# Conditioning vectors from VectorE sums over transposed weights, in a two-layer mLSTM / Mamba-2 / MoE step

## What is computed

```python
mod = silu(c) @ ada_w[l] + ada_b[l]      # (6 * 1024), for c and for c_ctx; l = 0, 1
x <- LayerNorm(ALPHA * x + gate * sublayer(x * (1 + scale) + shift))
```

## Time and profile before

| | us |
|---|---|
| median of 3 runs | 1399.95 |
| lowest, highest | 1393.66, 1410.97 |
| the profiled execution | 1397.49 |
| its span (first to last instruction) | 1395.7 |

### The profile page before, as it was taken

One profiled execution on the slowest core, in us unless ns is written; L12 is line 12 of the kernel. 1 busy time (PEld: TensorE's weight loads), 2 busy tenths in 40 slices (PEclk: granted clock), 3 DMA queues, 4 the chain that ended last, 5 costly groups with the idle time before them and its releaser, 6 DMA issues.

```text
span 1395.7 us, 15980 instructions
## 1 busy us (share of the span) xinstructions
PE 1263.1 (90%) x5974; PEld 687.4 (49%) x5974; DVE 526.4 (38%) x1263; ACT 352.2 (25%) x763; POOL 159.2 (11%) x222
## 2 busy tenths in 40 slices
PE   6999998999999999897779999999999999899573
PEld 3555555554566444643224555555666544644221
DVE  0344336432222122721013446557887222541014
ACT  1322332221310011211014132233555310311011
POOL 5000210000000000004003101003233000002201
PEclk9999997999999999899898999999999999899797
DMA  9566203337354552599949473234444266399934
GB/s 375 211 227 234 83 0 133 109 121 248 112 212 152 179 181 75 225 418 421 402 170 360 152 303 113 77 98 139 149 134 138 76 274 253 126 400 421 420 154 152
DMA packets 75416, 287.10 MB, mean 206 GB/s; under 512 B 7644, under 2 KB 18140, under 8 KB 61388
## 3 DMA queue, kind: packets, MB, share of 16 engines
q1 hardware_dynamic: 53472, 233.07, 44.5%
q10 hardware_dynamic: 17468, 37.67, 7.6%
q0 software_dynamic: 4400, 15.35, 2.8%
HBM read 258.16 MB, written 27.90 MB: 205 GB/s over the span
## 4 chain that ended last, share of the span: by engine, by line
PE 73%; DMA 9%; DVE 9%; issue 5%; ACT 3%; SPq 1%; ACTq 0%; POOL 0%; DVEq 0%; POOLq 0%
PE bank L586 21%; PE bank L608 12%; PE bank L747 7%; DMA arena<-in_moe_gu 4%; PE bank L959 4%; PE bank L767 3%; PE bank L559 3%; DMA ring<-in_ada_w 3%; PE bank L1155 3%; DVE arena L2478 2%; PE bank L995 2%; PE bank L890 1%; PE bank L987 1%; PE bank L850 1%; PE bank L546 1%
## 5 line engine op out<-in xcount | busy, mean ns | idle before, releaser
L586 PE MATMUL bank<-hT,ring 128*128 128x384 f32 x896 | 300.9, 494 | 3.8 <-ACT hT L1514 1.7
L586 PEld LDWEIGHTS bank<-hT,ring 128*128 128x128 f32 x896 | 169.9, 193 | 122.5 <-issue 13.6
L608 PE MATMUL bank<-ring,arena 128*128 128x512 f32 (+1 forms) x512 | 173.4, 605 | 2.1 <-DVE arena L2086 2.1
L747 PE MATMUL bank<-arena,hT 128*64 128x512 f32 x416 | 105.8, 628 | 35.8 <-DMA arena<-in_moe_gu 24.3
L608 PEld LDWEIGHTS bank<-ring,arena 128*128 128x128 f32 (+1 forms) x512 | 72.6, 194 | 92.9 <-issue 86.8
L1920 DVE SCALAR_TENSOR_TENSOR arena<-arena,par 128x388 f32<-128x388 f32 x160 | 99.8, 624 | 5.6
L1155 PE MATMUL bank<-hT,ring 128*128 128x384 f32 x256 | 97.2, 505 | 0.2 <-ACT arena L1528 0.2
L747 PEld LDWEIGHTS bank<-arena,hT 128*64 128x64 f32 x416 | 37.1, 144 | 92.9 <-issue 87.3
L559 PE MATMUL bank<-ring,csil 128*32 128x256 f32 x768 | 64.3, 450 | 20.0 <-DMA ring<-in_ada_w 12.4
L1461 POOL TENSOR_TENSOR arena<-arena 128x192 f32<-128x192 f32 x64 | 43.0, 702 | 240.0 <-PE bank L1188 156.6
L959 PE MATMUL bank<-ring,arena 128*128 128x512 f32 x128 | 58.9, 620 | 0.9 <-ACT arena L1591 0.9
(11 more groups left out here) (412 smaller groups left out, 1625.3 us busy)
## 6 DMA issues: line engine op xcount, KB each, us to landing
arena<-in_moe_gu SPq DMA_DIRECT2D x56, 1024.0 KB, 14.6
ring<-in_ada_w SPq DMA_DIRECT2D x96, 512.0 KB, 5.7
arena<-in_moe_dn SPq DMA_DIRECT2D x28, 1024.0 KB, 11.9
ring<-in_b_w_in SPq DMA_DIRECT2D x40, 512.0 KB, 4.2
ring<-in_a_w_in SPq DMA_DIRECT2D x32, 512.0 KB, 3.6
ring<-in_moe_gu SPq DMA_DIRECT2D x12, 1024.0 KB, 14.1
arena<-acs_rows ACTq DMA_DIRECT2D x32, 384.0 KB, 3.6
yg<-arena ACTq DMA_DIRECT2D x18, 512.0 KB, 8.4
```

The lines of the kernel that those rows point to most:

```text
L586: last = mm(keys[j][1][:, 0:T], w[:, k, P * j:P * j + P], hT[:, 4 * half + k, :], start=half == 0 and k == 0, stop=half == 1 and k == 3, s ...
L608: last = mm(keys[t][1][p:p + tokens.shape[1], :], tokens, w[:, j, :], start=k == 0, stop=k == KE - 1, skip_group_check=True)
L747: last = mm(ps[CAP * u:CAP * u + CAP, :], m_hg[:, q % 2, P * k + CAP * u:P * k + CAP * u + CAP], v3(w[u][1], 4)[:, j, :], start=k == 0, st ...
```

## The change

40 of the 48 units leave TensorE. Units 0 to 7 (columns 0 to 15 of layer 0) stay. The other 80 column blocks of 128 come as slabs of kind "column", from a copy of the weights laid out so that partition p holds the 1024 weights of column 128*j + p. VectorE multiplies a slab with silu(c), kept in all partitions, and sums it with one `scalar_tensor_tensor` with accumulator per vector: two instructions of 128x1024 per slab, each waited for. No PSUM, no copy of rows, no turn. `biased` adds bias and 1 afterwards.

silu(c) and silu(c_ctx) in all partitions (128 x 2048, 1 MB) are loaded three times (`c_rows_at`) by a broadcast load, once to a free region of the arena and twice to hT, and ScalarE applies Silu in place (`c_silu`). For the second and third the load stands on SyncE's queue until the last z projection has read hT.

The 80 columns are summed in three places: 20 in the xu stage, two after each of ten convolutions; 28 in the down stage, in one go after `diagonals(0)`; 32 in the out stage, as 8, 6 and 18, with `diagonals(2)` between and the mean-square wait ahead of the last 18. Their slabs stand between those of TensorE in the same ring, and their slots come free by a semaphore of VectorE. `gate_rows(0)` moves from after the eighth down slab to after the third, `gate_rows(2)` to after the sixth out slab (banks 5 and 7).

```diff
+        c_free = region(3 * D, KE * T + KE * W_PAD)[0]
+        hT_free = hT.rearrange("p k t -> p (k t)")
+        c_places = [(v3(a[:, 0:2 * D], 2), a[:, 2 * D:3 * D]) for a in (c_free, hT_free, hT_free)]
...
+        for tile in range(KD):
+            add("ada", ada_w, tile)
+        for i in range(2 * KD):
+            add("xu", a_in, i // 2, (i % 2,))
+            if i == 1:
+                c_rows_at.append(len(slabs))
+            if i in (1, 2, 4, 5, 7, 8, 10, 11, 13, 14):
+                add_columns(2)
...
         for s in range(8):
             for kp in range(2):
+                if s == 1 and kp == 0:
+                    c_rows_at.append(len(slabs))
                 slabs.append(("down", a_dn[s // 4, 2 * (s % 4) + kp]))
+                if s < 6:
+                    add_columns(4 if (s, kp) in ((1, 0), (2, 1)) else 2)
             prefetch(0, 4 + s)
...
+        rest_at = len(slabs) + RING
...
+        c_rows_at.append(len(slabs))
         for s in range(16):
             slabs.append(("out", b_dn[s // 8, s % 8]))
+            if s < 12:
+                add_columns(4 if s in (1, 3, 5, 7) else 2)
             if s >= 6:
                 prefetch(1, s - 6)
...
+        slab_free = {n: (sem("summed"), i + 1) for i, n in enumerate(column_slabs)}
...
-                    if with_ada:
-                        ada_slab()
...
-                if l == 0:
-                    ada_fill(4)
...
+            for t in range(NT):
+                turn_norm(1, t)
...
-                elif i == 1:
-                    ada_fill(4)
-                elif i == 2:
-                    ada_fill(4)
-                    ada_turn()
...
+                if n in c_rows_at:
+                    i = c_rows_at.index(n)
+                    sp.wait_ge(sem("c_in"), 16 * (i + 1))
+                    if i:
+                        sp.wait_ge(filled, group["in", (i + 1) * KE - 1][1])
+                    sp.dma_start(c_places[i][0].rearrange("p v k -> p (v k)"),
+                                 i_["c_rows"].to_broadcast([P, 2 * D])).then_inc(sem("c_in"), 16)
...
+            def c_silu(i):
+
+                act.wait_ge(sem("c_in"), 16 * (i + 2))
+                ac(c_places[i][0], c_places[i][0], ACT.Silu).then_inc(sem("csil_ready"), 1)
...
             z_silu(12, 15)
+            c_silu(2)
             new_state(6)
...
+            def summed(place, n):
+
+                rows, products = c_places[place]
+                dve.wait_ge(sem("csil_ready"), place + 2)
+                for _ in range(n):
+                    i = n_summed[0]
+                    n_summed[0] += 1
+                    at, (l, j) = column_slabs[i], divmod(2 * KD + i, 48)
+                    dve.wait_ge(slab_in[at % RING], landed[at])
+                    for v in range(2):
+                        ins = ve.scalar_tensor_tensor(out=products, in0=slot(at), scalar=1.0, in1=rows[:, v, :],
+                                                      op0=ALU.mult, op1=ALU.mult, accum_out=mod[:, l, j, v:v + 1])
+                        if not v:
+                            link(ins)
+                    ins.then_inc(sem("summed"), 1)
+                    dve.wait_ge(sem("summed"), i + 1)
...
+                if c in (1, 2, 4, 5, 7, 8, 10, 11, 13, 14):
+                    summed(0, 2)
+            biased(0, 16, 36)
...
             diagonals(0)
+            summed(1, 28)
+            biased(0, 36, 48)
+            biased(1, 0, 16)
             mixed(0, "yA")
...
+            summed(2, 8)
+            biased(1, 16, 24)
             for s in range(2):
                 dve.wait_ge(sem(f"out{s}"), 16 * (OUT_C + OUT_S))
+            diagonals(2, (0, 1))
+            summed(2, 6)
+            diagonals(2, (2, 3))
             ps = await_bank(dve, "single", 4)
             ve.tensor_scalar(rms, ps[:, 0:NT], float(D) / E2, EPS, ALU.mult, ALU.add).then_inc(read("single"), 1)
+            summed(2, 18)
+            biased(1, 24, 48)
             dve.wait_ge(sem("sqrt_ready"), 2)
             link(ve.reciprocal(rms, rms))
-            diagonals(2)
```

More of the change, by code:

```diff
@@ L336, in add, with add_columns @@
                 slabs.append((kind, w[q, tile]))
-        ada_at = [0]
-        def add_ada(n):
+        columns_at = [2 * KD]
+        column_slabs = []
+        def add_columns(n):
             for _ in range(n):
[L342 to L351, removed]
+                column_slabs.append(len(slabs))
+                slabs.append(("column", ada_wT[columns_at[0] // 48, columns_at[0] % 48]))
+                columns_at[0] += 1
+        c_rows_at = []
+        for tile in range(KD):
[6 more added lines that the diff above has]
+                add_columns(2)
         for h in range(H):
@@ L524, in slab @@
                 n = n_slab[0]
+                while slabs[n][0] == "column":
+                    n += 1
                 assert slabs[n][0] == kind, (n, slabs[n][0], kind)
@@ L1025, in _, with norm_steps @@
             head_back(KE - 1)
-            def norm_steps(n, more):
+            def norm_steps(n, rows_at, more):
                 def at(stage, i):
-                    if (stage, i) == (0, 7):
+                    if (stage, i) == (0, rows_at):
                         gate_rows(n)
@@ L1503, in ada_row @@
                     act.wait_ge(filled, group["turned", s - 2])
-                if s >= 24:
-                    act.wait_ge(read("ada"), s)
                 ac(ada_rows(s), ps[:, 0:256], ACT.Copy).then_inc(read("ada"), 1)
@@ L1551, in _ @@
             ac(a_u, a_u, ACT.Ln, bias=1.0).then_inc(sem("softplus_ln"), 1)
-            for s in range(24, 26):
-                ada_row(s)
             act.wait_ge(sem("gate_m"), 1)
@@ L1627, in modulated, with moe @@
                         ins.then_inc(sem("h_act"), 1)
-            def moe(l, unit):
+            def moe(l):
                 L = f"_{l}"
@@ L1710, in squared @@
                    scale=1.0 / D).then_inc(sem("std_ready"), 1)
+            rows_kept(0)
             norm(0)
-            moe(0, 28)
+            moe(0)
             rows_kept(1)
-            for s in range(29, 33):
-                ada_row(s)
             squared(1, 0)
@@ L1858, in _ @@
             norm(2)
-            moe(1, 47)
+            moe(1)
             rows_kept(3)
@@ L1971, in _ @@
             ve.tensor_scalar(a_nM, a_nM, -1.0, None, ALU.mult).then_inc(sem("gate_m"), 1)
-            for s in range(26, 28):
-                ada_row(s)
-            ada(2, 1, 0, 8)
             ps = await_bank(dve, "single", 1)
@@ L2100, in columns, with diagonals @@
                 link(ve.tensor_tensor(out=h_bias, in0=h_bias, in1=mod[:, lm, shift:shift + 8, :], op=ALU.add))
-            def diagonals(n):
+            def diagonals(n, parts=range(4)):
                 l, j = divmod(n, 2)
                 j = (16, 40)[j]
-                for k in range(4):
+                for k in parts:
                     v, half = divmod(k, 2)
@@ L2402, in moe @@
                 if l == 0:
-                    ada(4, 1, 10, 16)
                     columns(1)
```

147 lines of the change are left out of this document (47 added, 100 removed).

## The result

| | before | after |
|---|---|---|
| median, us | 1405.46 (of 4 runs beside it) | 1438.96 (of 4 runs) |
| lowest, highest | 1393.66, 1412.07 | 1434.47, 1444.22 |
| profiled execution, its span | 1397.49, 1395.7 | 1439.15, 1437.3 |

The changed kernel is slower: ratio 1.0249, 95% interval 1.0162 to 1.0336. Predicted was 1417, a loss of 20 us. The spans differ by 41.6 us, the medians by 33.5 (the profiled execution of before lay among its lower ones).

A forecast was written before the change was run, and what follows sets the result against it. TensorE bounds the kernel before (busy 90% of the span); VectorE becomes the bound in xu. Terms -1 + 0 - 26 + 21 + 24 + 2 = +20 on 1397.5 us give 1417.5, said as 1417; range 1390 to 1440.

The forecast's parts named there:

- A column at 2.52: VectorE's price of one column slab: two multiply-and-sum instructions at 1.26 us each, 2.52 us a column.
- The xbc gain: Layer 1 xbc projections: 14 units leave TensorE, first projection 8.3 us earlier, two gaps of 8.9 us go; -26 us.
- The stand of 13 before the fourth down slab: Down stage: TensorE, done with the gate rows at 486.6, stands until 499.5 for a slot held by the fourth column.
- rival 3: All column sums run at half rate by the skill's rule: 171 us more, about 1580 us; chance 0.02.
- 3.5 us from issue to landing plus 0.4 for the issue: Load time of a ring slab, used in the slab-by-slab walk of the stages; 3.9 us together.
- rival 2: The ring stutters: exposed loads take 4.9 us or more, TensorE's clock falls in gaps; +48 us, 1445; chance 0.2.
- from there it runs at 5.39 a slab: Down stage, after the stand ending at 499.5: TensorE keeps 5.39 us a slab, just about VectorE's pace.
- +21: Down stage, 28 columns: sums end at 556.1, last parts at 577.6 for 556.7; +21 us, bounds +12 to +26.
- +24: Out stage, 32 columns: waits for squares and loads, end at 1216 for 1192.4; +24 us, bounds +12 to +30.
- xu, -1 forecast: xu stage, 20 columns: 21.4 us off TensorE, VectorE the new bound, so 1 us gained; bounds -21 to +6.
- Clock, +2 forecast: Lower TensorE clock after two long stands, partly hidden: +2 us, bounds 0 to +6.
- L: Theory of the experiments: with columns between, the shared ring holds only one or two TensorE slabs, so loads come late.

The follow-up runs named there:

- Short sums: Changed kernel with every multiply-and-sum over the first 128 of 1024 weights, slabs loaded whole: xu 87.1 us, down 111.4, out 122.1; whole time can't be read.
- before with late expert loads: Kernel before, with only the expert loads of the down and out stages moved behind the last slab: 1408.50 us, ratio 1.0005.
- filling the stands: Changed kernel with products of no use in TensorE's two long stands, ahead of the fourth down and eighth out slab: 1436.86 us, ratio 1.0205.
- own slots: Changed kernel with order of waits moved and six separate slots for the 28 down column slabs: 1416.35 us, ratio 1.0095.

## Why the prediction was wrong

**Right, with their sizes.** A column at 2.52 (2.53). VectorE as the bound of xu (87.1 without its price, 104.0 with it). The xbc gain: the changed kernel is 36.3 us late at the mix of the experts (772.92 for 736.67), 28.8 at the first projection (794.30 for 765.50), 10.3 at the last: 26.0 in all. The next three projections of 32 stand in one piece, without gaps:

```profile
794.30 12.72 PE L580 MATMUL bank<-hT,ring 128*128 128x384 f32 x32 [0.65 <-ACT hT L1612]
812.25 31.23 PE L580 MATMUL bank<-hT,ring 128*128 128x384 f32 x96
```

The stand of 13 before the fourth down slab (12.39), VectorE's idle time ahead of the mean square (8.35) and the stand of 9 behind it (10.0).

The Trainium skill (Vector Engine (DVE) Microarchitecture Reference, Points that are easy to get wrong) would have the sums at half rate. The 120 of them into hT took 1224 ns on average, as the one row of before had said, so the trace again does not agree, and rival 3 is out.

**The steps that failed.** Two terms of the sum were too small, each for a cause of its own: the landing in down and out, and the clock in xu. First the landing: "3.5 us from issue to landing plus 0.4 for the issue", used for every load of the walk. It came from slabs of the xu stage, not of "the same stages" as I wrote against rival 2. The trace of before has these too, in its lists of DMA issues of the down stage (475 to 555) and of the out stage (1093 to 1193):

```profile
ring<-in_a_w_down SPq DMA_DIRECT2D x9, 512.0 KB, 3.5
...
ring<-in_b_w_out SPq DMA_DIRECT2D x10, 512.0 KB, 9.9
```

In the down stage 3.5 held for before, with expert loads on the same queue. In the out stage it did not, and TensorE never stood, because the ring was six slabs ahead: a late slab costs nothing there. In the changed kernel the down and out slabs landed in 5.5 and 6.4 us at the median, with up to three issues and 1 MB ahead of them, and now it costs. I named this as rival 2's condition and turned it down by that row. From it follows the second wrong sentence, "from there it runs at 5.39 a slab": it ran with stands of 5.25, 1.14, 1.29 and 1.37 more. Down was +25.9 for +21, out +30.2 with its start for +24.

**xu, -1 forecast, +5.8 measured** from the second gate product of the next stage on (160.52 for 154.72), and +6.8 up to the z products: with 7.8 us the largest miss of the sum. Here it was the slower product behind a stand, for which the sum had 2 us in the whole kernel and this walk nothing. VectorE's idle times while it waits for ScalarE's copy of a late slab were 3.05 and 3.00 us (at 72.90 and 114.06) where I had 1.8 each. The landing is not to blame: slabs of xu landed in 3.5 us at the median, and in the chain that ended last it is 3.44 with the issue, under my 3.9.

```profile
64.26 3.44 DMA ring<-in_a_w_in
...
67.74 4.56 PE bank L580 x8
```

A slab is half of two tiles, and the 8 records that end the first of them took 4.56 us; the next 8 took 2.58, by ScalarE's copies at 72.32 and 74.90. The granted clock was 0.61 and 0.65 from 67.7 to 72.3 and 1.00 after it, and 0.56 and 0.70 from 108.9 to 113.5, ahead of the other idle time. My walk had the full rate there: from the freed slot 3.9 + 2.6 + 0.6 for the copies, less the 5.6 us that VectorE still works, leaves 1.5, near my 1.8. Each time it is 2.0 us on the path of VectorE, which bounds the stage; the last convolution ended 4.0 us later than forecast (152.7 for 148.7), of which 0.7 is a later start of the stage. No run took this away by itself. Short sums show the whole price: 17 us of TensorE's 19.6 go to VectorE's pace, and its lag at the end (11.4 us from the last projection's start to the last convolution's end, 4.6 before) takes more than the rest.

**Clock, +2 forecast.** The products of z, down and out took 2.8, 4 and 5.4 us longer in sum than before, so as a count I was low, the two places in xu left aside. Of z's part some is not the change's: in before with late expert loads, which does not differ up to that place, the z stage took 91.9 us for 90.2. In out, filling the stands brought 1.0. After 2.60 us of waiting in xu 32 products took 12.28 us, after 2.73 us later on 10.56. The Trainium skill (TensorE: Matmul & The Clock Gate, HAM oscillation) says that load waits send the clock back again and again; this case shows it at some stands and not at others. After the second of these the granted clock was 1.00.

The sum by the measured terms: +6.8 up to the z products, +2.9 in them, +25.9, +0.7 for the experts of layer 0, -26.0, +30.2 for out with its start and +1.1 for the last experts, 41.6. Of the 21.6 us that my sum missed, 7.8 are xu's, 6.2 out's, 4.9 down's and 4.7 those of places that I had at nothing, less the 2 that I had put aside for the clock. Rival 2 (+48, 1445) comes nearest, with +6, +26 and +30 for xu, down and out. In down and out its mechanism is what happened, though more by the missing lead than by the clock. In xu its size is right by luck: it has loads of 4.9 us there, and they took 3.5.

**Open.** How L splits between the number of slots and the expert loads in the out stage, which had no own slots in any run; what the slower products after stands cost in xu and in down; and whether down with own slots would fall below 99 with the wait for the first own slab removed.

## What to carry to other kernels

A ring is a lead, not a buffer: before putting a second consumer's slabs into it, count how many slabs of the first it still holds and compare that time with a landing under the queue's full traffic, not with a landing that nobody waited for. A slab must not enter a shared ring before its consumer is near it; where a consumer has a long wait of its own, leave its slabs out of the ring until after it. Work that VectorE takes over belongs spread at the rate at which the stage leaves it idle: 80 columns in three dense blocks cost 2.5%; the same 80 at one or two for a slab, with the expert loads behind the last slab, gained 2.5%.

## What the hardware showed that I had not expected

Loads put off until after the last slab cost the experts nothing, though the expert stages move 421 GB/s without a gap (201.6 us for 202.2 from the first router product to the first xbc product). In layer 0 all but the last had landed when the router part began: DMA was busy for 0.98 of the down stage's last 20 us. In layer 1 they went on in it, where DMA was busy for 0.68 of 19 us; in the changed kernel it was busy there for 0.20. And the sum of 128x128 took 292 ns for 1224 of 128x1024, so that all but 0.16 us of a sum grows with its width.
